# A sum of P1 and P2 formed in one PSUM bank, and two weight sums of each unit made by an adding DMA transfer

## The reference, cut to what matters

```python
def _half_ffn(x, norm_g, w_gate, w_up, w_down):
    h = _rmsnorm(x, norm_g)
    return x + 0.5 * ((jax.nn.silu(h @ w_gate) * (h @ w_up)) @ w_down)
# one layer, d_model 1024, d_ff 2816, 536 tokens (16 meta, 512 prompt, 8 sample), float32:
x = _half_ffn(x, ffn1_norm, ffn1_w_gate, ffn1_w_up, ffn1_w_down)
u, q, k, v = _project(_rmsnorm(x, mix_norm), pos, w_in, q_norm, k_norm)
x = x + concat([_pool_mix(u, ...), _swa(q, k, v, sinks)]) @ w_out
x = _half_ffn(x, ffn2_norm, ffn2_w_gate, ffn2_w_up, ffn2_w_down)
```

## Time and profile before

| | us |
|---|---|
| median of 3 runs | 878.86 (878.55 to 878.98) |
| the profiled execution, first to last instruction (its span) | 877.7 |
| PE busy | 871.7 |
| DVE busy | 660.3 |
| ACT busy | 394.6 |
| POOL busy | 32.5 |
| granted clock of TensorE, mean | 0.998 of 2.4 GHz |
| 39 paired weight sums on DVE (L1591) | 47.4 |

### The profile page before, as it was taken

How to read it: one execution, slowest core, us unless ns; L and a number is a source line. 1 busy time by engine, 2 the same in 40 slices (tenths; PEclk the granted TensorE clock), 3 DMA queues, 4 the chain that set the end, 5 groups by cost and what they waited for, 6 DMA issues and landing times.

```text
span 877.7 us, 17077 instructions
## 1 busy us (share of the span) xinstructions
PE 871.7 (99%) x7086; PEld 857.1 (98%) x7086; DVE 660.3 (75%) x982; ACT 394.6 (45%) x642; POOL 32.5 (4%) x37
## 2 busy tenths in 40 slices
PE   9999999999999999999999999999999999999998
PEld 8999999999999999999888999999999999999998
DVE  7979557997569986755787697996479975799754
ACT  8635213554225553434754465554125542255420
POOL 0000000000000000013423000000000000000000
PEclk9999999999999999999999999999999999999999
DMA  8233413432424422522311405324233324333241
GB/s 297 72 126 127 133 49 121 126 116 86 144 91 139 123 74 84 194 73 74 117 47 62 151 31 169 120 78 166 83 121 120 121 85 145 113 122 126 85 122 61
DMA packets 43612, 98.57 MB, mean 112 GB/s; under 512 B 4336, under 2 KB 5488, under 8 KB 43536
## 3 DMA queue, kind: packets, MB, share of 16 engines
q1 hardware_dynamic: 41808, 95.01, 33.6%
q10 hardware_dynamic: 1728, 2.48, 0.8%
HBM read 93.53 MB, written 3.60 MB: 111 GB/s over the span
## 4 chain that ended last, share of the span: by engine, by line
PE 95%; DVE 2%; DMA 1%; ACT 1%; issue 1%; SPq 0%; DVEq 0%
PE ps L619 45%; PE ps L738 15%; PE ps L740 15%; PE ps L739 15%; PE ps L958 1%; PE ps L976 1%; PE ps L967 1%; DMA xT<-x 1%; PE ps L797 1%; PE ps L931 0%; DVE wlo L1535 0%; DVE sqx L1799 0%; PE ps L881 0%; DVE hlo L1662 0%; DVE hid L1655 0%
## 5 line engine op out<-in xcount | busy, mean ns | idle before, releaser
L738 PE MATMUL ps<-xhi,whi 128*128 128x260 f32 (+1 forms) x1092 | 310.2, 284 | 0.1
L740 PE MATMUL ps<-xhi,wlo 128*128 128x260 f32 (+1 forms) x1092 | 310.0, 284 | 0.0
L739 PE MATMUL ps<-xlo,whi 128*128 128x260 f32 (+1 forms) x1092 | 309.6, 283 | 0.0
L738 PEld LDWEIGHTS ps<-xhi,whi 128*128 128x128 f32 x1092 | 205.3, 188 | 0.8 <-issue 0.6
L740 PEld LDWEIGHTS ps<-xhi,wlo 128*128 128x128 f32 x1092 | 205.5, 188 | 0.0
L739 PEld LDWEIGHTS ps<-xlo,whi 128*128 128x128 f32 x1092 | 205.4, 188 | 0.0
L1606 DVE TENSOR_TENSOR wlo<-full,whi 128x1024 fp32r<-128x1024 f32 (+1 forms) x117 | 160.3, 1394 | 0.0
L1127 ACT CAST whi<-raw 128x1024 fp32r<-128x1024 f32 (+1 forms) x73 | 73.1, 1002 | 152.6 <-PE ps L619 146.1
L619 PE MATMUL ps<-hhi,whi 128*128 128x268 f32 (+1 forms) x690 | 140.4, 285 | 0.3
L619 PE MATMUL ps<-hlo,whi 128*128 128x268 f32 (+1 forms) x690 | 140.1, 284 | 0.0
L619 PE MATMUL ps<-hhi,wlo 128*128 128x268 f32 (+1 forms) x690 | 139.7, 284 | 0.0
(11 more groups left out here) (201 smaller groups left out, 1087.0 us busy)
## 6 DMA issues: line engine op xcount, KB each, us to landing
full<-gu SPq DMA_DIRECT2D x78, 512.0 KB, 4.5
raw<-d SPq DMA_DIRECT2D x32, 448.0 KB, 3.5
full<-gu SPq DMA_DIRECT2D x39, 256.0 KB, 2.7
raw<-d SPq DMA_DIRECT2D x16, 512.0 KB, 3.7
raw<-w_in SPq DMA_DIRECT2D x10, 512.0 KB, 3.6
raw<-gu SPq DMA_DIRECT2D x8, 512.0 KB, 4.2
raw<-w_out SPq DMA_DIRECT2D x8, 512.0 KB, 3.8
xT<-x SPq DMA_DIRECT2D x8, 268.0 KB, 5.0
```

The lines of the kernel that those rows point to most:

```text
L738: nc.tensor.matmul(dst, whi_t, xhi_t, start=(first and pr == 0), stop=False, skip_group_check=True)
L739: nc.tensor.matmul(dst, whi_t, xlo_t, start=False, stop=False, skip_group_check=True)
L740: last = nc.tensor.matmul(dst, wlo_t, xhi_t, start=False, stop=(pr == KC - 1), skip_group_check=True)
```

## The change

Two edits.

P1 is copied by ACT from its bank into P2's bank (`seed_p1` in place of `keep_p1`), and P2's first matmul no longer clears the bank, so P2 is added to what is there. DVE's addition falls away; `scale_gate0` is one multiplication. `p1c`, `p1_kept` and `c11_summed` are gone: P6 and P2 wait for `p1_seeded`, and the seed waits for the scaled gate of the unit before (`gate0_scaled`), which reads the bank. Before stage two's units one matmul is added that writes the bank's 260 columns.

The sums in slots 1 and 4 are made by a DMA transfer that adds blocks 0 and 3 from DRAM to block 2 in SBUF (512 KB more read for each unit). GpSimd issues it, when load c of that unit has landed (`add_blocks`). ACT's `hi_a` and DVE's `weight_sums` wait for its landing (`g_added`) in place of `added`.

```diff
-            first = name in ("P1", "P7", "P2")
+            first = name in ("P1", "P7")
...
-            pe.wait_ge(p1_kept, u + 1)
+            pe.wait_ge(p1_seeded, u + 1)
             unit_product(s, p, i, "P6")
 
         def p2(s, p, i):
-            u = unit_no(s, p, i)
-            if u:
-                pe.wait_ge(c11_summed, u)
+            pe.wait_ge(p1_seeded, unit_no(s, p, i) + 1)
             unit_product(s, p, i, "P2")
...
             act.wait_ge(a_loaded[i % 3], k)
-            act.wait_ge(added, unit_no(s, p, i) + 1)
+            act.wait_ge(g_added[i % 3], k)
...
-        def keep_p1(s, p, i):
+        def seed_p1(s, p, i):
 
             u, n = unit_no(s, p, i), STAGES[s]["n"]
             act.wait_ge(products, product_no(s, p, i, "P1"))
             if u:
-                act.wait_ge(c11_summed, u)
-            nc.scalar.copy(p1c[:, 0:n], chain_bank(s, p, i, n)).then_inc(p1_kept, 1)
+                act.wait_ge(gate0_scaled, u)
+            nc.scalar.copy(single_bank(n), chain_bank(s, p, i, n)).then_inc(p1_seeded, 1)
...
             dve.wait_ge(b_loaded[r], k)
-            dve.wait_ge(c_loaded[r], k)
-            nc.vector.tensor_tensor(full[:, r, 1:5:3, :], full[:, r, 1:5:3, :], full[:, r, 0:7:6, :], ALU.add
-                                    ).then_inc(added, 1)
-            dve.wait_ge(added, u + 1)
+            dve.wait_ge(g_added[r], k)
...
-            nc.vector.tensor_tensor(gate[:, cols], single_bank(n), p1c[:, 0:n], ALU.add).then_inc(c11_summed, 1)
-            dve.wait_ge(c11_summed, u + 1)
-            nc.vector.tensor_tensor(gate[:, cols], gate[:, cols], rstd[:, cols], ALU.mult).then_inc(gate0_scaled, 1)
+            nc.vector.tensor_tensor(gate[:, cols], single_bank(n), rstd[:, cols], ALU.mult).then_inc(gate0_scaled, 1)
...
     @block.gpsimd
     def _(pool):
+        def add_blocks(s, p):
+
+            for i in range(PARTS[s][p]):
+                f, r = AT[p] + i + (PLAIN[s] if p == 0 else 0), i % 3
+                src = a[f"gu{s + 1}"][:, f * 4 * BLK:(f + 1) * 4 * BLK].rearrange("p (b c) -> p b c", b=4)
+                pool.wait_ge(c_loaded[r], 16 * (uses_before(s, p, i) + 1))
+                pool.dma_start(full[:, r, 1:5:3, :], src[:, 0:4:3, :], accum_op=ALU.add).then_inc(g_added[r], 16)
+
+        for p in range(3):
+            add_blocks(0, p)
         pool.wait_ge(unit_done, U_IN)
...
         pool_lo(3)
+        for p in range(3):
+            add_blocks(1, p)
```

More of the change, by code:

```diff
@@ L198, in build @@
     upn, _ = place("upn", [P, NT])
-    p1c, _ = place("p1c", [P, NH_ALL])
     u2c, _ = place("u2c", [P, 2, NH_ALL])
@@ L375, in build @@
     c_loaded = [sem(f"c_loaded{r}") for r in range(3)]
-    added = sem("added")
+    g_added = [sem(f"g_added{r}") for r in range(3)]
     products = sem("products")
@@ L381, in build @@
     lo_ready = [sem(f"lo_ready{r}") for r in range(3)]
-    p1_kept = sem("p1_kept")
+    p1_seeded = sem("p1_seeded")
     u2_kept = sem("u2_kept")
     u4_kept = sem("u4_kept")
-    c11_summed = sem("c11_summed")
     gate0_scaled = sem("gate0_scaled")
@@ L725, in plain_products_2 @@
             pe.wait_ge(rstd_ready, 3)
+            nc.tensor.matmul(single_bank(n), xhi7[:, 0, 0:P], tokens(xhi7, 0, 0, n), start=True, stop=True)
         def unit_product(s, p, i, name):
@@ L1269, in part @@
                     hi_c(s, p, i)
-                keep_p1(s, p, i)
+                seed_p1(s, p, i)
                 if i + 1 < n:
@@ L1637, in scale_gate0 @@
             dve.wait_ge(products, product_no(s, p, i, "P2"))
-            dve.wait_ge(p1_kept, u + 1)
             if i:
```

## The result

The changed kernel takes 888.54 us (median of 4 runs, 887.67 to 891.03); the kernel before, timed beside it, 878.70 (878.25 to 878.98). The ratio is 1.0118, 95% interval 1.0105 to 1.013: slower by 1.2%, some 9.8 us. The forecast was 881.2, so the direction was right and the time lies at the upper edge of the whole range (877.8 to 889), but outside the forecast's own (879.5 to 884): the loss is four times the 2.3 us that I had summed up.

The account below looks back on a forecast made before the run. PE bounds the kernel (871.7 of 877.7 us busy), so only pauses count: 3.2 us of late sums, −1.0 for today's pauses, +0.1 for the added matmul give +2.3, 881.2 us; range 877.8 to 889, the forecast's own 879.5 to 884.

Parts of the forecast that it names:

- The seed: ACT's copy of P1 into P2's bank: up to 1.0 us more is hidden, worth 0; one added matmul costs 0.1 us.
- Steady units: Past a part's first units, the transferred sum has 11.5 us and more from load c's landing, so nobody waits.
- The pauses of before: PE idle before P5(0) in parts 2, 3, 5, 6, behind DVE's paired sum: 1.0 us together, at most won back.
- The 1.1 us ahead of the down products: PE's pause hanging on the last hidden tile's low part, which starts from P4's end; no edit shortens it.
- The rooms: Time from load c's landing until unit 1's sum delays P5(0): 6.3, 5.1, 5.9, 5.2 us in parts 2, 3, 5, 6.
- D: Time from load c's landing to the sum's landing: forecast 5.4 us, 6.6 in parts 2, 3 and 6.
- The base: Adding transfer without neighbours: 2.4 us fixed, 2.6 for data taken twice, 0.4 for issue, 5.4 in all.
- The estimate from the Trainium skill's two pages: GpSimd's transfer at 2.0 us plus 2.4 for data at half rate, 4.4 us; all six parts in time.
- The crowd: Unit 2's loads beside unit 1's transfer in parts 2, 3 and 6: half of 2.5 us added, 5.4 becoming 6.6.
- has about 8: Unit 2 of a part: about 8 us from load c's landing until its sum is due, so counted as covered.
- long transfer: Rival: GpSimd slow making 256 adding pieces, or these stand behind SP's loads; 7 to 10 us, 885 to 904; chance 0.20.
- nearest end, 888.7: Case with the transfer landing 7.6 us after load c in every part: +9.8 us, 888.7.

## Why the prediction was right in direction and wrong in size

**Right.** Nothing but pauses could be won: DVE lost 57.5 us and the steady step stayed at 0.122 us. (I had summed 47.4 and 17, or 64 us, and 1.6 us a unit; it was 1.3 to 1.5. That changes nothing, since nobody waits for it.) The seed is worth 0 (ratio 1.0006 alone). Steady units are covered: with 33 transfers and unit 1's sums on DVE, PE waits for none. The place was right, `hi_a` of unit 1 and behind it ACT's copy for P5(0), and the worst parts were 3 and 6. The pauses of before were the paired sum's: cutting it in two ended all four. The 1.1 us ahead of the down products stayed.

**The rooms** were right as well. With the D measured in each part (6.2, 7.1, 8.5, 6.4, 6.4, 8.4) against 5.4 or more, 6.3, 5.1, 7, 5.9, 5.2, parts 2 to 6 come to 0.8 + 3.4 + 0 + 0.5 + 3.2 = 7.9; the trace has 0.9, 3.3, 0, 0.5 and, before the clock fell, 3.4. Part 1, with no pause before, had a room given only as "5.4 or more": 6.2 cost nothing at P5(0).

**The term that failed is D**, 5.4 and 6.6 us by me, in both its pieces.

*The base*: 2.4 + 2.6 + 0.4 = 5.4, measured 6.2 without neighbours (0.3 until GpSimd starts, 5.9 to landing). Doubling the data was right in kind: the addition takes 2.1 times the engine time. The page of the Trainium skill cited for it ("Collectives: The Full Stack", "The bandwidth ceiling") has half the rate for an engine that adds. The trace agrees. But a plain transfer's data is 1.6 us on the engines, where I had read 1.3 from two loads that followed each other, and GpSimd's issue takes 1.20 us, where I had put SP's 0.4. Added one behind the other, these pieces (2.1 fixed, 3.4 of data, 0.8 more of issue, 0.3) would make 6.6; which of them overlap in the measured 6.2, no run shows. The estimate from the Trainium skill's two pages, 4.4 us, missed by more: by it all parts were in time.

*The crowd*: I took half of the 2.5 us that load a of part 2 once suffered, in parts 2, 3 and 6. In parts 3 and 6 SP's next loads start 0.8 and 0.6 us after GpSimd, and D was 2.3 and 2.2 us above 6.2. In parts 1, 2 and 5 they start 1.8, 1.8 and 1.6 us after it, and D was 0, 0.9 and 0.2 above. This order could be read before: there unit 2's loads start 1.1 and 1.0 us after c's landing in parts 3 and 6, but 2.2 in part 2, which I had put with them. Yet the distance alone doesn't settle it: in part 2 D was 6.1, 7.1 and 8.6 in three kernels in which the loads came 1.6 to 1.8 us behind GpSimd. The half was without ground. Taking the full 2.5, with the base as it was, gives 7.9 in parts 2, 3 and 6, and 1.6 + 2.8 + 2.7 − 0.9 = +6.2, 885.1 us.

Of the 7.5 us between the forecast loss and the measured one, D's size makes 4.7 (7.9 us late in place of 3.2). The rest was not in the sum at all.

**Not foreseen.** First, unit 2 of a part "has about 8" of room. In part 1 its own load c took 6.6 us instead of 3.7, and then D was 8.6: the sum landed 11.5 us after c's usual landing and was 1.0 us late, so that the room was in fact some 10.5 and still didn't hold. The slow load is the work of unit 1's adding transfer: in the kernel that has unit 1's sums on DVE the same load took 3.6. I had looked only at what the neighbours do to the new transfer, not at what it does to them. Second, the clock: a pause of some 3 us can be followed by 3.4 us at 1.2 GHz, which cost 1.6 us in part 6, P1(1) included. The sum with the old rooms, 7.9 + 1.0 (P5(1)) + 1.6 (the clock) + 0.1 (P1(1) of part 2) + 0.1 (the added matmul) − 1.0 = 9.7, closes against the 9.8 measured.

**The rival "long transfer"** with D from 7 to 10 was right for three parts of six (7.1, 8.5, 8.4), for its second reason (standing beside SP's loads), not for the first. That the time nearly equals its nearest end, 888.7, and so lies just inside the range, is luck: that sum has D = 7.6 in all six parts and neither the clock nor unit 2. The Trainium skill's page "SBUF — State Buffer" ("Who interferes with whom") has some modes of DVE keep GpSimd from writing descriptors, and a two-input TENSOR_TENSOR not. The trace agrees as far as it can: with such instructions on DVE, GpSimd's took 1.19 to 1.33 us at all 39 places.

What stays open: why the clock fell behind a pause of 2.31 us in one execution and not behind 3.04 in another, why D in part 2 differs so much between kernels, and how often a cut transfer is late.

## What to carry to other kernels

When work goes from an engine that nobody waits for to a transfer, the busy share that it frees is worth nothing; what decides is the narrowest place, so list the room of every start and compare it with the transfer's longest landing beside its neighbours, not with the median. Count in both directions: a new transfer between two bursts of loads is slowed by them and slows them. If only a part of its result is needed first, cut it there, or keep the one early unit in each part on the engine; both brought all 9.8 us back here, and neither beat the kernel before.

## What the runs showed of the hardware

- An adding transfer of 512 KB from DRAM issued by GpSimd lands after 6.1 us, a plain one after 3.9; one from SP after 3.7. The addition takes 2.1 times the engine time, and GpSimd's instruction 1.20 instead of 0.72 us.
- Loads queued beside it make it up to 2.4 us longer; alone on the queue all six landed in 5.6 to 5.9 us. It slows them too: a load of 512 KB took 6.6 us beside it, 3.6 without.
- ACT copies 128x260 or 128x268 from one PSUM bank into another in 0.36 to 0.39 us, as long as the same copy into SBUF (0.38):

```profile
L1206 ACT COPY ps<-ps x39: 360/389/394, 57.8 to 832.3; 128x260 f32<-128x260 f32 x21, 128x268 f32<-128x268 f32 x18
```

- After pauses of 2.3 to 3.5 us TensorE ran 3.4 us at 1.2 GHz in six cases of seven (idle time 2.31, 2.51, 2.99, 3.25, 3.36 and 3.54 us; not after 3.04). A stretch of this kind stands in the profiled execution of before as well, at 428 us, with no pause of that length ahead of it, and not in that of the seed-only kernel; their spans differ by 1.4 us (877.7 and 876.3).
